# Ten units of a gated feed-forward projection computed from seven half products each

## The reference

```python
h2 = rmsnorm(x, norm_ffn[l])
gate, up = jnp.split(h2 @ w_ffn_in[l], 2, axis=-1)      # w_ffn_in: 1024 x 5632
x = x + (jax.nn.silu(gate) * up) @ w_ffn_out[l]         # w_ffn_out: 2816 x 1024
```

## Time and profile before

| | us |
|---|---|
| median of 3 runs | 1322.49 |
| profiled execution | 1322.59 |
| its span (first to last instruction) | 1320.8 |
| PE busy | 1309.5 |
| DVE busy | 766.8 |
| ACT busy | 568.5 |
| POOL busy | 338.2 |
| first FIN unit starts, second projection starts | 400.61, 646.48 |

### The profile page before, as it was taken

How to read it: one execution, slowest core, us unless ns; L and a number is a source line. 1 busy time by engine, 2 the same in 40 slices (tenths; PEclk the granted TensorE clock), 3 DMA queues, 4 the chain that set the end, 5 groups by cost and what they waited for, 6 DMA issues and landing times.

```text
span 1320.8 us, 21121 instructions
## 1 busy us (share of the span) xinstructions
PE 1309.5 (99%) x8097; PEld 1087.5 (82%) x8097; DVE 766.8 (58%) x1485; ACT 568.5 (43%) x785; POOL 338.2 (26%) x95
## 2 busy tenths in 40 slices
PE   8999999999999999999999999999999999999997
PEld 6888989888888888888888888777788888888886
DVE  4763462864456766666744480344497778845336
ACT  5744253361344222222223252555565565654333
POOL 6421222234333000000134404422211112124441
PEclk9999999999999999999999999999999999999999
DMA  6232322214235555555432343333223222223321
GB/s 198 88 96 64 95 83 76 84 61 160 96 96 144 142 139 142 139 140 138 122 110 88 108 104 109 97 100 91 64 66 92 69 66 69 93 66 105 117 96 65
DMA packets 199638, 134.56 MB, mean 102 GB/s; under 512 B 5719, under 2 KB 190920, under 8 KB 199574
## 3 DMA queue, kind: packets, MB, share of 16 engines
q1 hardware_dynamic: 198342, 131.41, 34.2%
q10 hardware_dynamic: 848, 1.60, 0.3%
q0 software_dynamic: 384, 0.64, 0.2%
HBM read 131.51 MB, written 2.12 MB: 101 GB/s over the span
## 4 chain that ended last, share of the span: by engine, by line
PE 98%; DVE 1%; ACT 0%; DMA 0%; issue 0%; ACTq 0%; DVEq 0%
PE acc L494 22%; PE acc L496 22%; PE acc L495 22%; PE acc L503 3%; PE acc L505 3%; PE acc L504 3%; PE acc L518 1%; PE acc L517 1%; PE acc L519 1%; PE acc L2642 1%; PE acc L2641 1%; PE acc L2640 1%; PE acc L2495 1%; PE acc L2496 1%; PE acc L2497 1%; PE mid L2540 1%
## 5 line engine op out<-in xcount | busy, mean ns | idle before, releaser
L472 POOL TENSOR_TENSOR wlo<-raw,whi 128x2048 fp32r<-128x2048 f32 (+1 forms) x74 | 323.2, 4368 | 945.1 <-ACT whi L468 945.0
L494 PE MATMUL acc<-hhi,whi 128*128 128x512 f32 x896 | 353.8, 395 | 0.0
L495 PE MATMUL acc<-hlo,whi 128*128 128x512 f32 x896 | 349.4, 390 | 0.0
L496 PE MATMUL acc<-hhi,wlo 128*128 128x512 f32 x896 | 349.3, 390 | 0.0
L468 ACT ACTIVATE whi<-raw 128x2048 fp32r<-128x2048 f32 (+1 forms) x108 | 199.7, 1849 | 106.6 <-PE acc L496 90.3
L496 PEld LDWEIGHTS acc<-hhi,wlo 128*128 128x128 f32 x896 | 168.3, 188 | 35.5
L494 PEld LDWEIGHTS acc<-hhi,whi 128*128 128x128 f32 x896 | 168.4, 188 | 34.4 <-issue 0.9
L495 PEld LDWEIGHTS acc<-hlo,whi 128*128 128x128 f32 x896 | 168.5, 188 | 33.5 <-issue 0.2
L1274 DVE TENSOR_TENSOR wlo<-raw,whi 128x2048 fp32r<-128x2048 f32 (+1 forms) x34 | 76.5, 2250 | 21.9 <-ACT whi L468 21.9
L503 PE MATMUL acc<-hhi,whi 128*128 128x512 f32 x160 | 65.5, 410 | 0.0
L494 PE MATMUL acc<-ahi,whi 128*128 128x512 f32 x165 | 64.5, 391 | 0.0
(11 more groups left out here) (418 smaller groups left out, 2356.5 us busy)
## 6 DMA issues: line engine op xcount, KB each, us to landing
raw<-in_w_in_dram SPq DMA_DIRECT2D x56, 512.0 KB
raw<-in_w_in_dram SPq DMA_DIRECT2D x26, 1024.0 KB
raw<-in_w_ffn_in_dram SPq DMA_DIRECT2D x44, 512.0 KB
ada<-in_w_ada_dram SPq DMA_DIRECT2D x24, 512.0 KB, 3.8
raw<-in_w_ffn_out_dram SPq DMA_DIRECT2D x16, 704.0 KB
raw<-in_w_out_dram SPq DMA_DIRECT2D x8, 1024.0 KB
xnat<-in_x_dram SPq DMA_DIRECT2D x8, 512.0 KB, 6.0
raw<-in_w_branch_gla_dram SPq DMA_DIRECT2D x4, 1024.0 KB
```

What stands on the lines that cost most here:

```text
L472: nc.gpsimd.tensor_tensor(wlo[:, slot, 0:n], raw[:, slot, 0:n], whi[:, slot, 0:n].bitcast(f32), ALU.subtract).then_inc(s_unit_lo, 1)
L494: nc.tensor.matmul(acc[bank][:, :], h, xh[:, k, :], start=(k == 0), stop=False)
L495: nc.tensor.matmul(acc[bank][:, :], h, xl[:, k, :], start=False, stop=False)
L496: last = nc.tensor.matmul(acc[bank][:, :], lo, xh[:, k, :], start=False, stop=(k == nk - 1))
```

## The change

The 22 units are now 11 pairs. Of each pair the even unit (plain) is computed as before; the odd one, in pairs 1 to 10, by seven products in the place of eight. A unit's product is taken as a 2 x 2 block product: weights by feature halves and by gate and up, the normed x by feature halves and token halves (`EARLY`, `LATE`, 256 tokens each). Four sums of weight blocks (`weight_sums`, on DVE) and four sums of token blocks (`token_sums`, on DVE, made once during the U_OUT units) give the seven products P1 to P7 (Winograd's form); each has 4 slices, three matmuls each, of 256 columns. So a unit has 84 matmuls of 128 x 256 in the place of 48 of 128 x 512. Three additions happen in PSUM (P2 onto P1, P4 onto P7, P3 onto P5), the others on DVE (`comb_v` to `comb_12`), and these must have read the bank before PE adds to it. Pair 0 has two plain units, which PE runs first.

What else moves with it:
- The token sums need the full-precision normed x (`h_half`, eight more ACT copies) and their own high and low parts (`t_hi`, `t_lo`). The buffer `h_second` lies where `ada` lies, so SP waits for all four `t_lo` before it loads `ada`.
- The low parts of the FIN weights are made by DVE in six or eight smaller steps per pair; POOL makes those of units 0 and 1 only. The multiplication of `ada` by silu(c) goes from DVE to ACT, and 12 of the 24 one-column matmuls go from the first projection to the second.
- The result `a` is kept in full (`fa`), and `ahi`, `alo` of all 22 slices are made at the end of the projection.
- The first group of the second projection takes weights by halves: the first 11 slices for two output blocks, then the other 11.

The core of the diff:

```diff
                 ada_load(j, j)
-            with sp.Fori(1, FT // 2) as i:
-                for j in range(2):
-                    load_pair(U_FIN + j + i * 2, j, w_fin, i * 256 + j * P, i * 256 + j * P + D_FF)
-                    ada_load(i * 2 + j, j)
...
+            def gate_up_load(i, j):
+                for n in range(2):
+                    sp.dma_start(rawk(j, KT, 2 * P, n * P, P), kview(w_fin, i * 256 + (j * P + n * D_FF), P))\
+                        .then_inc(s_unit_in[j], 16)
...
+            def pair_load(i, j):
+                if j == 0:
+                    sp.wait_ge(s_q_lo, i * 2 + (Q_LO0 - 2))
+                else:
+                    sp.wait_ge(s_w_lo, i * 6 + (W_LO0 - 12 + MADE[P1]))
+                gate_up_load(i, j)
...
+            for j in range(2):
+                sp.wait_ge(s_unit_lo, U_FIN + j + 1)
+                gate_up_load(1, j)
+            ada_load(2, 0)
...
@@ -846,6 +952,10 @@
             def head_split(h, j):
                 v = U_HEAD + 1 + j
                 split_hi(act, v + h * 4, (v + 1) % 2, lin=first_tile(v - 1) + h * 8, head=True)
+
+            def token_sum_hi(n):
+                act.wait_ge(s_t, T0 + KT // 2 + 3 * (n + 1))
+                A(t_hi[:, :, n, :], t_full[:, :, n, :], ACT.Copy).then_inc(s_t_hi, 1)
...
+                        token_sum_hi(k - KT // 2 - 2)
...
+            def half_hi(i, n):
+                if n == 0:
+                    act.wait_ge(s_unit_in[0], fin_loaded(i))
+                if isinstance(i, int) and i == 1:
+                    act.wait_ge(s_prod, quarter_done(0, 2 * n + 1))
+                else:
+                    act.wait_ge(s_prod, prod_done(i - 1, (P6, P5)[n]))
+                A(quad(whi, 2 * n, 2), quad(raw, 2 * n, 2), ACT.Copy).then_inc(s_q_hi, 1)
...
+            def seven_unit(i):
+                block_hi(i, P5)
+                gate_sigmoid(i * 2)
+                p6_out(i)
+                half_hi(i + 1, 0)
+                half_hi(i + 1, 1)
+                gate_out(i)
...
+            split_hi(act, U_FIN + 1, 1)
+            token_sum_hi(2)
+            token_sum_hi(3)
+            half_hi(1, 0)
             norm_rs(0)
-            ffn_split(0, 1)
-            ffn_tile(0, 0)
-            ffn_tile(0, 1)
-            with act.Fori(1, FT // 2) as i:
-                for j in range(2):
-                    ffn_split(i, j)
-                    ffn_tile(i, j)
+            half_hi(1, 1)
...
+            def token_sums(k):
+                first = h_half[0][:, k % 4, :]
+                t1, t2, t3, t4 = (t_full[:, m, k % 4, :] for m in range(4))
+                dve.wait_ge(s_h_full, H_FULL0 + k + 1)
+                if k < KT // 2:
+                    V.tensor_tensor(t1, first[:, LATE], first[:, EARLY], ALU.subtract).then_inc(s_t, 1)
+                    return
+                second, done = h_half[1][:, k % 4, :], T0 + KT // 2 + 3 * (k % 4)
+                V.tensor_tensor(t3, second[:, LATE], first[:, LATE], ALU.subtract).then_inc(s_t, 1)
+                dve.wait_ge(s_t, done + 1)
+                V.tensor_tensor(t2, t3, first[:, EARLY], ALU.add).then_inc(s_t, 1)
+                dve.wait_ge(s_t, done + 2)
+                V.tensor_tensor(t4, second[:, EARLY], t2, ALU.subtract).then_inc(s_t, 1)
...
+            def token_sum_lo(n):
+                dve.wait_ge(s_t_hi, T_HI0 + n + 1)
+                V.tensor_tensor(t_lo[:, :, n, :], t_full[:, :, n, :], t_hi[:, :, n, :].bitcast(f32), ALU.subtract)\
+                    .then_inc(s_t_lo, 1)
...
@@ -1571,47 +1797,196 @@
                 dve.wait_ge(s_norm_hi, nth(1) + k + 1)
                 V.scalar_tensor_tensor(hlo[:, k, :], xres[:, k, :], vcol[:, R_NF + k:R_NF + k + 1],
                                        hhi[:, k, :].bitcast(f32), ALU.mult, ALU.subtract).then_inc(s_norm_lo, 1)
-
...
+            def weight_sums(i):
+                a11, a21, a22, a12 = w_part(0, 0), w_part(1, 0), w_part(1, 1), w_part(0, 1)
+                s1, s3, s2, s4 = (by_k(fs[:, n, :]) for n in range(4))
+                dve.wait_ge(s_unit_in[1], fin_loaded(i))
...
+            def comb_v(i):
+                dve.wait_ge(*handed_on(i, R6))
+                V.tensor_tensor(fv[:, :], fc6[:, :], acc[R1][:, 0:H], ALU.add).then_inc(s_comb, 1)
+
+            def comb_w(i):
+                dve.wait_ge(s_prod, prod_done(i, P7))
+                dve.wait_ge(s_comb, i * 4 + (COMB0 - 4 + 1))
+                V.tensor_tensor(fw[:, :], fv[:, :], acc[R7][:, 0:H], ALU.add).then_inc(s_comb, 1)
...
+            def seven_out(i):
+                dve.wait_ge(s_f_sig, i * 2 + 2)
+                dve.wait_ge(s_comb, i * 4 + (COMB0 - 4 + 4))
+                V.tensor_tensor(cols(fa, i * 2 + 1), fup[:, :], fn[:, :], ALU.mult).then_inc(s_f_a, 1)
+
+            def plain_norm(i):
+                dve.wait_ge(s_norm_rs, 1)
+                dve.wait_ge(s_prod, quarter_done(i, 3))
+                if later(i):
+                    dve.wait_ge(s_f_a, i * 2 + F_A0)
+                V.tensor_tensor(fn[:, :], M[0][:, :], nrs[:, :], ALU.mult).then_inc(s_f_norm, 1)
+
+            def plain_gate(i):
+                dve.wait_ge(s_f_sig, i * 2 + 1)
+                V.tensor_tensor(fn[:, :], fn[:, :], M[0][:, :], ALU.mult).then_inc(s_gmul, 1)
+
+            def plain_out(i):
+                dve.wait_ge(s_gmul, i + 1)
+                V.tensor_tensor(cols(fa, i * 2), fn[:, :], M[1][:, :], ALU.mult).then_inc(s_f_a, 1)
...
+            def second_out():
+                dve.wait_ge(*handed_on(0, R1))
+                V.tensor_tensor(fa[:, 1, :], fn[:, :], acc[R6][:, :], ALU.mult).then_inc(s_f_a, 1)
...
+            def seven_unit(i, slot):
+                block_lo(i, P5)
+                if isinstance(i, int) and i == 1:
+                    second_out()
+                else:
+                    seven_out(i - 1)
+                plain_norm(i)
+                plain_gate(i)
+                plain_out(i)
+                comb_v(i)
+                half_lo(i + 1, 0)
+                comb_w(i)
+                comb_22(i)
+                half_lo(i + 1, 1)
+                ada_sum(i, slot)
+                comb_21(i)
...
+            unit_pairs(U_BR, U_FIN)
+            split_lo(pool, U_FIN, 0)
+            split_lo(pool, U_FIN + 1, 1)
             pool.wait_ge(s_unit_lo, U_FOUT + 2)
             unit_pairs(U_FOUT + 2, U_VAL, FT // 2 * P)
...
+            def product(i, m):
+
...
+                    pe.wait_ge(s_t_lo, T_LO0 + KT // 2)
+                for k in range(KT // 2):
+                    if m in (P2, P4):
+                        ws = slice((2 * k + (m == P4)) * P, (2 * k + (m == P4) + 1) * P)
+                        w_hi, w_lo = quad(whi, P2, 2)[:, ws], quad(wlo, P2, 2)[:, ws]
...
+                        w_hi, w_lo = quad(whi, m)[:, ws], quad(wlo, m)[:, ws]
+                    xh, xl = token_part(m, k)
+                    mm(o, w_hi, xh, start=(m in (P1, P6, P7, P5) and k == 0), stop=False, skip_group_check=True)
+                    mm(o, w_hi, xl, start=False, stop=False, skip_group_check=True)
+                    last = mm(o, w_lo, xh, start=False, stop=(k == KT // 2 - 1), skip_group_check=True)
...
+            def plain_unit(i, slot):
+                if later(i):
+                    pe.wait_ge(s_f_a, i * 2 + (F_A0 - 1))
+                else:
+                    pe.wait_ge(s_unit_lo, U_FIN + 1)
+                    pe.wait_ge(s_x_res, 6)
...
+                    if later(i) and k % 4 == 0:
+                        pe.wait_ge(s_q_lo, i * 2 + (Q_LO0 - 1 + k // 4))
+                    if not later(i):
+                        pe.wait_ge(s_norm_lo, nth(1) + k + 1)
+                    for j in range(2):
+                        ws = slice((2 * k + j) * P, (2 * k + j + 1) * P)
+                        mm(M[j][:, :], whi[:, 0, ws], hhi[:, k, :], start=(k == 0), stop=False)
+                        mm(M[j][:, :], whi[:, 0, ws], hlo[:, k, :], start=False, stop=False)
...
+            def seven_unit(i):
+                for m in range(7):
+                    if m in (P1, P6, P7, P5):
+                        pe.wait_ge(*handed_on(i - 1, R_OF[m]))
+                        if isinstance(i, int) and i == 1 and m == P6:
+                            pe.wait_ge(s_f_a, F_A0 + 2)
+                    else:
+                        pe.wait_ge(s_comb, i * 4 + (COMB0 - 4 + {P2: 1, P4: 2, P3: 3}[m]))
...
+                    seven_unit(h * 2 + n)
+            plain_unit(PAIRS - 1, 0)
+            seven_unit(PAIRS - 1)
 
             def ffn_out(i, j):
                 half = FT // 2
-                ks = slice(j % 2 * half, (j % 2 + 1) * half)
+                first = not later(i)
                 pe.wait_ge(s_unit_lo, i * 4 + U_FOUT + j + 1)
-                if j < 2:
-                    pe.wait_ge(s_f_lo, (j + 1) * half)
-                tile(U_FOUT, j, j % 2, 0, 4, i, nk=half, ncol=P, xh=ahi[:, ks, :], xl=alo[:, ks, :])
+                b, _, free = TL(U_FOUT, j, 4, i)
+                pe.wait_ge(s_acc_free[b], free)
```

(60 more changed lines are left out.)

384 lines of the change are left out of this document (300 added, 84 removed).

## The result

The changed kernel takes 1337.72 us (median of 4 runs, 1337.15 to 1338.63) against 1322.42 for the kernel before: a ratio of 1.0116, 95% interval 1.0104 to 1.0129. It is slower by 15.3 us where 6.7 was forecast, and 1337.72 lies outside the range of 1320.0 to 1334.5. The profiled execution took 1337.62 us, with a span of 1335.3.

A forecast was written before the change was run, and what follows sets the result against it. The prediction took TensorE's consecutive matmuls as the bound. Terms -10.5 + 2.9 + 8.5 + 2.5 + 0.5 + 0.85 + 1.9 = +6.65 on 1322.59 gave 1329.2 us, range 1320 to 1334.5.

The forecast's parts named there:

- Gain on PE: From third unit to second projection, ten plain and ten seven-product units take 212.0 us in place of 222.5: -10.5.
- Moved adaptation matmuls: The 12 ada matmuls leaving the first projection come back in the second at 0.24 us each: +2.9.
- Start of the third unit: Weight loads wait behind ada loads and t_lo, so the third unit starts at 432.4, not 423.94: +8.5 us.
- Clock: TensorE runs slower after the 9 us idle before the third unit: +2.5 us, bounds 0 to 2.5.
- Inside a seven-product unit: P2 and P4 fit with 0.2 us to spare, nine times: +0.5 us in all, bounds 0 and 4.5.
- P6 of pair 1: P6 waits once for the bank holding unit 1's up result until second_out, behind P5's low part: +0.85 us.
- End of the projection: The second projection's first tile waits 1.7 us for alo slices, and the last unit's P2 0.2: +1.9 us.
- 1 (the load isn't late): Third unit's weights arrive in time, it starts 0.5 earlier and the clock stays: 1317.7 us, chance 12%.
- 3 (P2 late each time): Start as forecast, but P2 is late by 0.5 us in each of nine units: 1333.2 us, chance 14%.
- Rival 2: POOL doesn't hold up DVE: third unit's start costs +4.3, about 5 us idle, no lost clock: 1322.5 us, 14%.

The follow-up runs named there:

- the best version: The changed kernel with third unit's loads first, adaptation sum early, two small reorderings, and low parts of three weights moved from GpSimd to VectorE: 1315.81 us, ratio 0.9951.
- the version with DVE's low parts: Changed kernel, third unit's loads first, adaptation sum early, two small reorderings, low parts of the second projection's third and fourth weights on VectorE: 1318.60 us, ratio 0.9970.
- adaptation matmul later: Changed kernel with third unit's loads first, plus the second projection's first-group adaptation matmul behind slice 10 of a tile, not slice 5: 1324.92 us, ratio 1.0027.
- loads first: Changed kernel with the third unit's weight loads issued ahead of the wait for t_lo and the first two ada loads: 1326.80 us, ratio 1.0035.
- adaptation sum early: Changed kernel with VectorE forming the second-to-last adaptation sum after the low part of slice 17, not behind all 22: 1338.38 us, ratio 1.0112.

## Why the prediction was wrong, point by point

The direction was right and the size too small, by 8.6 us. By its steps:

- **Gain on PE, -10.5: right.** In the best version the stage takes 9.95 less. The period of a pair is 21.23 us in the changed kernel (463.96 to 506.42 is two pairs), against 21.20 from the terms. The 0.120 us of the earlier trace rows and not 0.113 was the right pace.
- **Moved adaptation matmuls, +2.9: right.** In the version with DVE's low parts PE's adaptation matmuls of the second projection stand 7.73 us apart, 0.25 over the 7.48 of a bare tile. The best version's stretch from the second projection to the end is 3.6 longer than before: this, 0.4 of wait for a weight's low part, and 0.3 unassigned.
- **Start of the third unit, +8.5: right in mechanism, 2.2 too small** (434.65 for 432.4). `t_lo` ended at 417.0 for 415.4, because the additional `h_half` copies delay ACT's split of an earlier unit (393.84 for 391.84); POOL's operation begins at 395.83 and no longer at 393.82, and holds a DVE add for 4.23 us in the place of 2.24. The prediction walked DVE only from 399.66 on and kept everything before it as it was. The load took 9.5 us from the issue to ACT, 0.8 more than taken. The chain of conversions behind it took 8.1, as walked. POOL's low part of the second unit, which the walk had just in time, is 1.5 us late; behind the later load this costs nothing.
- **Clock, +2.5: mechanism right, size 1.6**; but it fell a second time, which wasn't forecast. The 2.5 was borrowed from the kernel's start, where the granted clock read 1.00, so nothing ties that row to the clock, and that the size came near is luck. That the clock would fall, and to half rate, was an estimate; no row of the kernel before shows it. The runs do: behind the idles of 9.5 and 3.8 us the granted clock reads 0.50 and 0.51, and matmuls of 512 columns start 0.427 us apart in the place of 0.227.
- **Inside a seven-product unit, +0.5: right.** Only the last unit's P2 is late, by 0.26, behind an `alo`, so the small slack held in the others. P6 of pair 1 costs 0.94, for 0.85.
- **End of the projection, +1.9: right for the first tile, and here is the step that failed.** In that tile 1.5 us were lost to `alo`, and 0.3 before P2. But "The other eleven slices have a whole tile (7.5 us) more and are hidden, and so is ACT's work" asked only whether PE waits for these slices. It doesn't. It waits for what stands behind them on DVE: the adaptation sum, for a matmul that the change itself had moved into this stretch; and of the time by which DVE is late, 4.3 us are GpSimd's hold-up. With two of GpSimd's operations given to DVE no wait for a sum is left (1318.60 against 1324.95 us). The wait costs 3.8 us of idle and, from 675.19 to 680.39, twelve matmuls at low clock: 5.2 us for 2.7. Together 6.3, nearly three quarters of the miss. What it needed was there: the low parts' 0.61, GpSimd's operations of the second projection in the trace before (3.2 to 3.7 us each from 655.78 on), and the hold-up, which was taken into account at the start and not at the end.

Sum of the misses: 2.2 - 0.9 + 6.3 = 7.6 of 8.6; 0.5 lie outside the span (2.3 to 3.0 us in the changed kernel's runs, 1.8 before), and what makes them is open; the rest is in the small terms.

Of the rivals, 1 (the load isn't late) and 3 (P2 late each time) didn't happen. Rival 2 (POOL doesn't hold DVE) didn't either, and its price had an error that the runs showed: that an idle of about 5 us loses no clock was an estimate, and with that hold-up away the idle is 3.9 us and the clock falls to 0.50 all the same. The 14% for it was too much for a mechanism that the earlier trace rows had in plain sight.

What GpSimd's operation costs DVE is measured: 4.75 us for an add that begins 0.09 after GpSimd's operation, 0.43 without it; 3.27 us for a final step of 128 columns, 0.29 undisturbed. Why the two don't run side by side there, no run shows.

## What to carry to other kernels

When work is added to an engine's list, walk on to every instruction behind it, and ask of each who waits for it: the added work can be hidden and what it pushes back need not be. A wait that only moves when one edit removes it belongs to a backlog; look for the rate (here another engine's operation that holds this one up for 3 us at a time), not for the next instruction to reorder. And price a stall of TensorE with what follows it: here idles of 3.8 and 3.9 us cost 1.6 to 2.9 us more.

## What the runs showed of the hardware that I had not expected

- Giving GpSimd's work to the busier engine made that engine faster: two subtractions of 1408 columns cost DVE 1.6 us each, but it lost about 3 us to each while GpSimd made them (a final step of 0.29 us took 3.27). Total effect 6.3 us, with the waits and the clock behind them.
- The clock's fall doesn't need the long idle: after 3.9 us three matmuls ran at full pace and then the slow ones came, at a granted clock of 0.50, at the same total price (215.29 against 215.24 us for the stage, 213.68 with the idle filled). Nor does the price follow the idle's length. Matmul time lost to the low clock behind idles of 2.16 us (adaptation matmul later), 3.76 (second projection, loads first), 9.28 (adaptation sum early) and 9.45 us was about 1.7, 2.9, 2.7 and 1.6 us. An idle of 2.44 us ahead of the second unit (its low part on VectorE) cost nothing, at a granted clock of 1.00 behind it.
- A float32 matmul of the identity on 128 columns leaves two records, 0.113 us apart: 40 calls left 80 and filled 9.09 us.
